# Seven raw slots instead of five given over to upper parts in the last ten steps, and splits made up to six pairs ahead

## The reference

```python
def reference(x, ...):
    h = rms_norm(x, norm_mix)
    x = x + pool_mixer(h, pool_w, pool_scale)
    x = x + hier_moe(rms_norm(x, norm_ffn), ...)   # 4 groups x 8 experts, top 2 of one group
    return rms_norm(x, norm_final)

def expert_block(args):                # a block of 128 rows and its expert e
    xblk, e = args
    g_part, up = jnp.split(xblk @ w_gu[e], 2, axis=-1)     # 1024 -> 2 x 512
    return (jax.nn.silu(g_part) * up) @ w_dn[e]            # 512 -> 1024
```

## Time and profile before

| | before |
|---|---|
| median of three runs | 683.81 us (683.39 to 685.05) |
| profiled execution, first to last instruction (its span) | 681.9 us |
| what lies around the span, by the median | 1.9 us |
| PE busy | 659.4 us, 97% |
| DVE busy | 606.9 us, 89% |
| ACT busy | 527.7 us, 77% |
| moved by DMA | 242.62 MB, mean 356 GB/s |
| granted TensorE clock, mean | 0.993 |

### The profile page before, as it was taken

One profiled execution on the slowest core, in us unless ns is written; L12 is line 12 of the kernel. 1 busy time (PEld: TensorE's weight loads), 2 busy tenths in 40 slices (PEclk: granted clock), 3 DMA queues, 4 the chain that ended last, 5 costly groups with the idle time before them and its releaser, 6 DMA issues.

```text
span 681.9 us, 10290 instructions
## 1 busy us (share of the span) xinstructions
PE 659.4 (97%) x3638; PEld 556.6 (82%) x3638; DVE 606.9 (89%) x470; ACT 527.7 (77%) x446; POOL 238.3 (35%) x194
## 2 busy tenths in 40 slices
PE   6899989999999999999999999999999999999993
PEld 4899978888888888888888888888888888888872
DVE  6886789899888888889999889988889989898987
ACT  6995527887777778777777788778878888888894
POOL 3000020144444444444444333344333445452401
PEclk9999989999999999999999999999999999999998
DMA  8997869999999999999999999994999999999875
GB/s 296 418 419 254 274 186 421 410 366 377 388 382 382 373 382 378 376 380 380 371 380 389 374 396 382 402 372 158 340 364 380 387 379 378 386 377 389 289 293 202
DMA packets 45155, 242.62 MB, mean 356 GB/s; under 512 B 9719, under 2 KB 10879, under 8 KB 20546
## 3 DMA queue, kind: packets, MB, share of 16 engines
q1 hardware_dynamic: 34322, 220.39, 82.7%
q0 software_dynamic: 10800, 21.80, 11.6%
HBM read 230.34 MB, written 29.36 MB: 381 GB/s over the span
## 4 chain that ended last, share of the span: by engine, by line
PE 88%; DVE 5%; ACT 3%; DMA 2%; issue 2%; POOL 0%; SPq 0%; ACTq 0%; DVEq 0%; POOLq 0%
PE psum L1516 74%; PE psum L1536 4%; PE psum L1444 3%; PE psum L1547 2%; PE psum L1430 2%; PE psum L1462 2%; DMA pw_in<-in_pool_w 1%; DVE raw L1339 1%; PE psum L1453 1%; DMA out<-raw 1%; ACT end_junk L727 1%; DMA xg<-normed,src_all 1%; DVE pw L1037 0%; PE psum L1506 0%; DVE x_rest L999 0%
## 5 line engine op out<-in xcount | busy, mean ns | idle before, releaser
L1083 DVE TENSOR_TENSOR w_lo<-raw,w_hi 128x2048 fp32r<-128x2048 f32 x152 | 345.6, 2291 | 32.6 <-ACT w_hi L795 32.3
L795 ACT ACTIVATE w_hi<-raw 128x2048 fp32r<-128x2048 f32 x152 | 287.9, 1914 | 26.8 <-PE psum L1516 26.8
L1516 PE MATMUL psum<-w_lo,x_hi 128*128 128x512 f32 x616 | 182.8, 392 | 0.0
L651 POOL DMA_INDIRECT total<-ysb,dst_now x29 | 60.6, 2088 | 225.6 <-ACT ysb L875 225.6
L1516 PEld LDWEIGHTS psum<-w_lo,x_hi 128*128 128x128 f32 x616 | 115.1, 188 | 24.9 <-issue 0.5
L1516 PE MATMUL psum<-w_hi,x_hi 128*128 128x512 f32 x408 | 129.5, 399 | 0.0
L1516 PE MATMUL psum<-w_hi,x_lo 128*128 128x512 f32 x408 | 126.1, 390 | 0.0
L1083 DVE TENSOR_TENSOR w_lo<-raw,w_lo 128x2048 fp32r<-128x2048 f32 x40 | 89.9, 2288 | 5.4 <-ACT w_lo L795 5.3
L1516 PE MATMUL psum<-w_lo,h_hi 128*128 128x512 f32 x312 | 92.9, 393 | 0.5 <-DVE h_lo L1288 0.5
L1516 PEld LDWEIGHTS psum<-w_hi,x_lo 128*128 128x128 f32 x408 | 76.6, 188 | 16.8
L1516 PEld LDWEIGHTS psum<-w_hi,x_hi 128*128 128x128 f32 x408 | 72.9, 188 | 16.7 <-DVE w_lo L1083 3.5
(11 more groups left out here) (156 smaller groups left out, 772.5 us busy)
## 6 DMA issues: line engine op xcount, KB each, us to landing
raw<-in_expert_w_gu SPq DMA_DIRECT2D x128, 1024.0 KB, 7.9
raw<-in_expert_w_down SPq DMA_DIRECT2D x64, 1024.0 KB, 7.1
res<-in_x SPq DMA_DIRECT2D x8, 512.0 KB, 9.8
normed<-nx POOLq DMA_DIRECT2D x8, 512.0 KB, 7.5
total<-res SPq DMA_DIRECT2D x8, 512.0 KB, 8.8
raw<-total SPq DMA_DIRECT2D x8, 512.0 KB, 9.2
out<-raw SPq DMA_DIRECT2D x8, 512.0 KB, 3.9
pw_in<-in_pool_w SPq DMA_DIRECT2D x1, 1024.0 KB, 7.7
```

The costliest lines, as they stand in the source:

```text
L651: pool.indirect_dma_start(out=total[:, :], out_offset=bass.IndirectOffsetOnAxis(ap=dst_now[:].bitcast(u32), axis=0), in_=ysb[:], in_offset ...
L795: nc.scalar.activation(hi_at(s0, j), raw[q][:], ACT.Copy).then_inc(hi_done, 1)
L1083: V.tensor_tensor(w_lo[q][:], raw[q][:], hi_at(s0, j).bitcast(f32), ALU.subtract)\
L1516: last = mm(dst[:, n * N:(n + 1) * N], a[:, ch, :], b[:, c * D + n * N:c * D + (n + 1) * N], start=(ch == 0 and a is hi and b is b_hi), st ...
```

## The change

Two numbers. `SPARE` is 7 instead of 5: from pair 130 on there are 11 raw slots (instead of 13) and 10 places for upper parts (instead of 8). `ahead` grows by three in four steps instead of by one in two, and ends at 6 instead of 4.

```diff
@@ -57,7 +57,7 @@
     FREE_STEP = E - 10
-    SPARE = 5
+    SPARE = 7
@@ -374,7 +374,7 @@
         def ahead(s0):
-            return min(max(0, (s0 - FREE_STEP) // 2), 4)
+            return min(max(0, (s0 - FREE_STEP) * 3 // 4), 6)
```

## The result

The changed kernel took 686.1 us in the median of five runs (684.55 to 687.54), against 683.81 before: 1.0027 times as long, 95% interval 1.0015 to 1.0039. The profiled execution has a span of 684.4 us, 2.5 more than the 681.9 before.

The account below looks back on a forecast made before the run. PE, busy 97% of the span, was taken to bound the steps; earlier splits could win only in the last 35 us. Terms 0.45 + 0.34 = 0.8 us took 683.81 to 684.6 us, range 683.2 to 686.6.

Parts of the forecast that it names:

- (a): Steps 24 to 30: seven splits in six steps instead of four would not delay hid increasingly; 0 us, bounds 0 to 0.2.
- (b): Step 30: with two raw slots fewer, pair 189's load lands late, delaying hid and PE; +0.45 us, bounds 0 to 2.15.
- (c): At the end: squares wait for the slot of pair 185 instead of 183; +0.34 us, bounds 0.3 to 0.4.
- (d): At the end: tiles of the sum load some 5 us later but still before their squares; 0 us.
- three signs of being wrong: Squares starting before pair 185 is used, a step before 30 over 17.9 us, or the end moved over 2 us.
- The growing delay: Steps 25, 26, 29, 30: DVE's seven subtractions make hid 1.6 us later each; PE waits 6.4 us, 691 us; chance 0.07.
- Loads too late: Step 30: loads landing in 8.7 us or later make PE wait for hid; 686.3 us at 8.7; chance 0.08.
- No wait for the load: Step 30: landing under 6.5 us leaves only the slot's 0.34 us; 684.15 us; chance 0.15.
- The free slot: At the end: squares start at 649.45 without waiting for the slot; gain at most 1.9 us, 681.9 us; chance 0.06.

Follow-up runs that it names:

- lead_only: Changed kernel with SPARE back at 5 (13 raw slots, 8 places), so against the kernel before only the new lead up to six; ratio 1.0034.
- lead_five: Changed kernel (SPARE 7, eleven raw slots) with the lead capped at five instead of six; ratio 1.0010 to the kernel before.
- six_six: Changed kernel with SPARE 6 (12 raw slots, 9 places) instead of 7, lead up to six; ratio 0.9986 to the kernel before.
- scratch_moved: Changed kernel with the squares' scratch and the last hid's split in the oldest place for upper parts; ratio 0.9999 to the kernel before.
- tile_ahead: six_six_scratch with tile 3's squares and scaling put before the silu of expert 31; ratio 0.9976, 681.92 us against 683.91 for the kernel before.
- slots_only: Changed kernel with the old lead (up to four), so against the kernel before only the slots differ (SPARE 7); ratio 1.0008.
- six_six_scratch: Changed kernel with the edits of six_six and scratch_moved together; ratio 0.9991 to the kernel before.
- tile_only: Kernel before (SPARE 5, lead up to four) with only the tile order of tile_ahead; ratio 1.0014.
- before_again: Kernel before, unedited, timed against itself; ratio 0.9995.

## Why the prediction was right

**What bounds the kernel.** Right: A lies between 157.41 and 157.50 in every profile but those of the changed kernel, with its late load, and of lead_only, with its missing places. One reading was off: not every step takes 17.7 to 17.8 us. Steps 24 to 29 take 17.76 to 17.78 in every profile, but steps 22 and 23 take 17.87 to 17.91, before and after alike.

**(a) The row of steps with seven subtractions: 0.** Right, and shown by lead_five, six_six, scratch_moved and tile_ahead (A 157.41 to 157.50). The argument from the row at 574.17, that ACT sets the restart and the delay does not grow, held.

**(b) The load of pair 189: +0.45.** The mechanism is right. The size is 0.46 in the first profile, 0.19 in the second and 0 in scratch_moved's, with landings of 7.1, 6.8 and 6.6 us, so the 6.5 us from which the term was to begin hold too. That other landing times would change the term one for one was in its bounds; that they differ from run to run, so that the term is rather 0 to 0.5 than 0.45, was not said. The agreement of 0.46 with 0.45 is in part luck.

**(c) The slot of the squares: +0.34.** Right: 0.35, to be read alone in slots_only, where it passes in full into C (12.30 to 12.65). scratch_moved shows the cause by taking it away.

**(d) The tile loads: 0.** Right: no square waits for a tile in the kernel after, and the load of pair 191, which came late, held up nothing.

**The sum.** 0.8 us by the forecast, 0.8 and 0.5 us in A to D. The first timing, 2.3 us between the medians, was three times the forecast; in the profiled execution what was over, 1.6 us, lies before the first changed instruction. That it left 686.1 inside the range, and not above it, is luck. The second timing gave 1.0011, 0.75 us. Both intervals share 1.0015 to 1.0020; taken together the kernel is a little slower, and 0.3% was the bound below which I had called that no change. The spread of the medians I had put at half a us; the start makes more of it. Of the three signs of being wrong that the prediction named, one came up: the end of the profiled execution moved by 2.5 us, over the 2 us. That is the start again, for which this sign left no room. The other two did not come: the squares start at 655.37 us, behind pair 185 (655.35), and no step from 22 to 29 takes longer than 17.89 us.

**The rivals.** The growing delay: refuted by lead_five. Loads too late: its mechanism is real, its size was not reached. No wait for the load: refuted in both profiles of the changed kernel, but the 6.6 us in scratch_moved's profile are all but that case. The free slot, made true in scratch_moved, six_six and tile_ahead: I had put it at -1.9 us at most. The step of it that failed is the release of the third scatter: it waits for POOL's two before it and they for the store, so freeing the squares alone brings 0.8 us (six_six), and the tile order another 0.8.

## What to carry to other kernels

When buffers are handed from one stage to another, ask of both users when they get them: here ten steps of splitting ahead were bought with slots, and the price was in the last slot of a quite different user, the scratch of the end. A lead, the slots that feed it and the slots it fills have to be changed together; 13/8 with a lead of six lost to missing places, 11/10 to late loads and a late slot for the scratch, 12/9 gained. And time freed on an engine beyond what the waits behind it need is worth nothing (six_six_scratch against six_six) until work is moved into it (tile_ahead), while a move without the free time costs (tile_only).

## What the runs showed of the hardware

**A short wait may cost twice.** In lead_only a wait of 2.69 us at PE's weight load (PE's matmuls stand still for 2.27) was followed by 3.4 us at the lower clock level, which cost about 1.5 us more in the middle of the steps. PE had been at the full clock since 12 us. In the kernel after, the lower clock at 98.34 us likewise came straight behind a wait of PE, of 2.14 us for the gathered rows. But waits of 2.12 to 2.18 us at the same place in slots_only, lead_only and scratch_moved were not followed by it, and in the profile before it began at 91.72 us with no wait of PE over 1.25 us in the 70 us ahead of it. The Trainium skill (TensorE: Matmul & The Clock Gate, "Part 1: The HAM clock gate") says that the clock is gated by how busy PE has been lately; two events here agree with that in direction, and the others show that the length of one wait does not tell whether the clock falls.

**Where the lower clock falls at the start changes from run to run.** The kernel runs into the same waits of the router each time, and in the profiles the lower level stood at 91.7 to 95.1 us (before), at 98.3 to 101.8 (after), at 33.3 to 36.7 and again at 94.7 to 98.1 (before_again), for 6.8 us from 91.9 (tile_ahead), or, as in slots_only and scratch_moved, nowhere between 13 and 600 us. Where it falls on work with a wait behind it, it is free; in the kernel after it fell on products, and about 1.1 us were lost there. Profiles of one and the same kernel differ by 1.4 and 1.6 us in the start, twice what the change did; only stretches read from behind that point told the kernels apart.

**How long a load takes under load.** 1 MB, up to four under way, gathers and scatters beside it: 7.3 us in the median in the kernel after, from 5.1 to 9.4, over the 45 of its 55 loads whose landing the trace gives. Where in that range a single load falls was not explained.
